# The u and gate projections of a two-block model by one level of Strassen's scheme on one NeuronCore

## What is computed

```python
h = rms_norm(x, norm_gain[l])
proj = jnp.einsum('bsd,de->bse', h, w_in[l])          # 1024 -> 4352
q, k, v, z_attn, u_ssm, z_ssm, g = jnp.split(proj, SPLITS, axis=-1)
g_attn, g_ssm = jnp.split(g + b_gate[l], N_BRANCHES, axis=-1)
attn = windowed_gqa(q, k, v, ...) * jax.nn.silu(z_attn)
y = s5_bidirectional(u_ssm, ...)                       # 32 groups of 16 channels, state 64
y = gelu(y); y = y * sigmoid(y @ w_glu + b_glu); ssm = y * silu(z_ssm)
merged = sigmoid(g_attn) * (attn @ w_branch_attn) + sigmoid(g_ssm) * (ssm @ w_branch_ssm)
```

## Time and profile before

| | us |
|---|---|
| time, median of 3 runs (lowest to highest) | 3565.43 (3548.24 to 3568.06) |
| span of the profiled execution | 3566.1 |
| PE busy | 3443.9 (97%) |
| DVE busy | 1675.5 (47%) |
| ACT busy | 1038.4 (29%) |
| POOL busy | 1101.7 (31%) |
| mean granted clock of PE | 0.988 |

### The profile page before, as it was taken

The page is one execution under the profiler, slowest core; times in us unless marked ns, Lnnn a source line. Parts: engine busy times, 40 slices in busy tenths (PEclk is TensorE's granted clock), DMA queues, the critical chain, the costliest instruction groups (busy, mean ns, idle before and its releaser), DMA issues.

```text
span 3566.1 us, 32570 instructions
## 1 busy us (share of the span) xinstructions
PE 3443.9 (97%) x11216; PEld 1789.2 (50%) x11216; DVE 1675.5 (47%) x3818; ACT 1038.4 (29%) x2575; POOL 1101.7 (31%) x1493
## 2 busy tenths in 40 slices
PE   6999899999999999999999999999999996999998
PEld 5744455555544644444444444555665443444443
DVE  5675633334365474325565556754454554222222
ACT  3221222211110362002234445643332222222222
POOL 1477777400000393000000001765561101443442
PEclk9999999999999999999999999999999998999999
DMA  4234445433245112222221000000102225968885
GB/s 162 78 105 160 145 156 163 141 125 109 96 176 178 52 37 83 88 106 102 71 96 36 24 12 12 1 1 1 71 24 76 98 96 201 355 195 264 256 251 137
DMA packets 122506, 404.74 MB, mean 113 GB/s; under 512 B 20246, under 2 KB 47766, under 8 KB 107967
## 3 DMA queue, kind: packets, MB, share of 16 engines
q1 hardware_dynamic: 85036, 228.52, 18.7%
q0 software_dynamic: 31392, 153.50, 13.8%
q10 hardware_dynamic: 5904, 20.56, 1.6%
HBM read 340.28 MB, written 117.42 MB: 128 GB/s over the span
## 4 chain that ended last, share of the span: by engine, by line
PE 84%; DVE 9%; DMA 3%; ACT 3%; issue 1%; POOL 0%; SPq 0%; DVEq 0%; POOLq 0%; ACTq 0%
PE pst L142 65%; PE pst L147 6%; DVE arena L164 5%; PE pst L2294 3%; PE pst L2389 3%; PE pst L2297 2%; DMA pwd<-arena 2%; PE pst L1354 1%; PE pst L1269 1%; PE pst L828 1%; DVE arena L167 1%; DVE arena L170 1%; ACT arena L153 1%; ACT arena L1295 0%; PE pst L2536 0%
## 5 line engine op out<-in xcount | busy, mean ns | idle before, releaser
L142 PE MATMUL pst<-arena 128*128 128x512 f32 (+4 forms) x6570 | 2688.4, 566 | 11.0 <-ACT arena L153 3.8
L142 PEld LDWEIGHTS pst<-arena 128*128 128x128 f32 x6570 | 1242.5, 195 | 1285.8 <-issue 1217.4
L164 POOL TENSOR_TENSOR arena<-arena 128x4 f32<-128x4 f32 (+7 forms) x784 | 401.8, 512 | 81.4 <-DVE arena L2098 20.9
L164 DVE TENSOR_TENSOR arena<-arena 128x512 f32<-128x512 f32 (+9 forms) x791 | 377.9, 478 | 84.2 <-ACT arena L2335 20.4
L147 PE MATMUL pst<-arena 128*128 128x128 f32 x2144 | 321.7, 284 | 56.6 <-DVE arena L256 15.3
L147 PEld LDWEIGHTS pst<-arena 128*128 128x128 f32 x2144 | 255.6, 145 | 232.5 <-issue 151.7
L1322 POOL TENSOR_SCALAR arena<-arena 128x384 f32<-128x384 f32 (+1 forms) x128 | 151.4, 1200 | 543.1 <-DVE arena L1314 541.7
L2278 POOL TENSOR_SCALAR arena<-arena 128x512 f32<-128x512 f32 (+3 forms) x160 | 218.7, 1386 | 147.5 <-DVE arena L164 137.1
L153 ACT ACTIVATE arena<-pst,arena 128x128 f32<-128x128 f32 (+1 forms) x630 | 232.0, 465 | 95.7 <-PE pst L147 93.2
L167 DVE TENSOR_SCALAR arena<-arena 128x1 f32<-128x1 f32 (+9 forms) x605 | 164.0, 271 | 178.3 <-DMA arena<-in_bc 79.5
L152 ACT ACTIVATE arena<-pst 128x512 f32<-128x512 f32 (+4 forms) x250 | 124.6, 518 | 323.9 <-PE pst L142 197.5
(11 more groups left out here) (214 smaller groups left out, 2245.3 us busy)
## 6 DMA issues: line engine op xcount, KB each, us to landing
arena<-in_w_ada SPq DMA_DIRECT2D x48, 512.0 KB, 4.8
rotd<-arena POOLq DMA_DIRECT2D x32, 512.0 KB, 4.0
arena<-rotd SPq DMA_DIRECT2D x32, 512.0 KB, 4.6
arena<-sgd SPq DMA_DIRECT2D x16, 1024.0 KB, 6.9
arena<-pwd SPq DMA_DIRECT2D x32, 416.0 KB, 5.8
arena<-in_x SPq DMA_DIRECT2D x18, 512.0 KB, 4.4
pwd<-arena SPq DMA_DIRECT2D x16, 576.0 KB, 6.1
h2d<-arena SPq DMA_DIRECT2D x17, 512.0 KB, 2.9
```

Of the source, the lines that this page charges most:

```text
L142: x = t.do.matmul(o, l, r, start=(i == 0), stop=(i == len(pairs) - 1))
L164: own(v, s).tensor_tensor(o, a, b, op).then_inc(*inc(s, *event))
```

## The change

Weights of u and gates are laid out together (2560 columns, `w_ug`, ten pieces of 256 columns x 1024 rows). A round q of the new loop takes one such piece and a pair of token tiles (512 tokens of either half of the sequence): its 2 x 2 blocks of halves are multiplied with seven products of 4 matmuls (`te_st_product`) in place of eight. There are SQ = 20 rounds: ten for the first pair of token tiles and ten for the second. DVE makes four sums of weights in a round (S1 to S4), once for each pair of token tiles 16 sums of tokens (T1 to T3, N4, in TS), and the five additions that join the products (u2, u3, c22, c12, c21). ACT copies P1 (p1), evicts the first output block and does what was done for the gates. The first two pieces of each ten are u: it is stored to `ud` in memory, ordered by token place, and loaded into Ug by 32 DMAs of SP (`sp_ug`), which replaces the 64 transposes. The blocks of the norm are now done in the order 0, 2, 1, 3, the last three between the products of rounds 0 and 1. The parameters, the eight passes of `ve_mat` (each cut in three steps) and the lag steps stand as side steps 2q and 2q + 1 in DVE's round (`ve_side`). MAT_AT gives the first side step of each pass; the lag of a pass follows one round after its end. Banks 0 to 5 hold products, 6 and 7 the side work. In S5 only the 32 z tiles are left as filler: one at its start, 29 over its 128 places, two at its end.

```diff
-PRE, PRE2 = 64, 32
-LAG_AT = [0, 4, 9, 14, 18, 22, 27]
+SP_, UT = 10, 4
+SQ = 2 * SP_
+MAT_AT = [8, 11, 15, 18, 22, 25, 29, 32]
...
+        def te_st_product(t, q, name):
...
+            if name in FIRST:
+                t.wait_ge(*st_bank_free(q, i))
+            if name == "P2":
+                t.wait_ge(*at("st_ac", "p1", q))
+            if name == "P3":
+                t.wait_ge(*at("st_ve", "S4", q))
+                t.wait_ge(*at("st_ve", "c22", q))
+            if name == "P4":
+                t.wait_ge(*at("st_ve", "u3", q))
+                t.wait_ge(*at("st_ve", "N4", c, 3))
...
+        def te_st(t):
+            te_norm_first(t)
+            for q in range(SQ):
+                te_st_product(t, q, "P1")
+                if q == 0:
+                    te_st_product(t, q, "P2")
+                    te_norm(t, 2, 0, 8)
+                if q == 1:
+                    te_norm(t, 3, 0, 2)
+                te_st_product(t, q, "P5")
+                if q == 1:
+                    te_norm(t, 3, 2, 4)
+                te_st_product(t, q, "P6")
+                if q < 2:
+                    te_norm(t, (1, 3)[q], (0, 4)[q], (2, 6)[q])
+                te_st_product(t, q, "P7")
+                if q < 2:
+                    te_norm(t, (1, 3)[q], (2, 6)[q], (4, 8)[q])
+                if q:
+                    te_st_product(t, q, "P2")
+                te_st_product(t, q, "P3")
...
+                te_st_product(t, q, "P4")
...
+                if q == 1:
+                    te_bias_row(t)
+                if q in (2, 3):
+                    te_bias(t, q - 2)
+                if q in LAG_AT:
+                    te_lag(t, LAG_AT.index(q))
...
+            for q in range(SQ):
...
+                ve_st_u2(v, q)
...
+                ve_st_c22(v, q)
...
+                if q == SP_ - 1:
+                    ve_st_T1(v, 1, 0, 4)
+                    ve_st_T2(v, 1, 0, 4)
+                    ve_st_T3(v, 1)
+                if q + 1 < SQ:
+                    ve_st_sums(v, q + 1)
+                ve_side(v, 2 * q)
+                ve_st_c12(v, q)
...
+                ve_st_c21(v, q)
...
+                if q == SP_ - 1:
+                    ve_st_T4(v, 1)
+                ve_side(v, 2 * q + 1)
...
+        def ve_side(v, s):
+
+            if s == 1:
+                ve_bias(v)
+            if s == 2:
+                ve_prm_angle(v)
+            if s == 4:
+                ve_prm_coef(v)
+            if s == 5:
+                ve_prm_powers(v)
+            if s == 6:
+                ve_prm_turns(v, 0, 6)
+            if s == 7:
+                ve_prm_turns(v, 6, 11)
+            for q4 in range(8):
+                if s == 2 * LAG_AT[q4] + 2:
+                    ve_lag(v, q4)
+            for q4 in range(8):
+                if 0 <= s - MAT_AT[q4] < 3:
+                    ve_mat(v, q4, s - MAT_AT[q4])
...
+        def sp_ug(s):
+
+            for m in range(4):
+                for c in range(2):
+                    for j in ((1, 2), (3, 0))[m % 2]:
+                        s.wait_ge(*at(f"st_pg{j}", "st", SP_ * c + m // 2))
+                s.wait_ge(*at("st_pe", ("P5", "P6", "P7", "P4")[m], SQ - 1))
                 for k in range(8):
...
+        LAG_AT = [(m + 2) // 2 + 1 for m in MAT_AT]
...
+            for i in range(4 * G + 1):
+                acc += 1 if i == 0 else 29 / (4 * G)
```

More of the change, by code:

```diff
@@ L292, in build @@
-        Ug = reg(64, G, 256)
[L293 to L319, removed]
@@ new lines, in tok, with st_bank, st_released, st_bank_free @@
+        def tok(c, half):
+            return slice(1024 * half + 512 * c, 1024 * half + 512 * c + 512)
+        def st_bank(q, i):
+            return bank((4 * q + i) % 6)
+        def st_released(q, i):
+            return at("st_ac", "C11", q) if i == 0 else at("st_ve", ("c12", "u2", "c21")[i - 1], q)
+        def st_bank_free(q, i):
+            n = 4 * q + i - 6
+            if n >= 0:
+                return st_released(n // 4, n % 4)
+            return hT_evac(2, 6) if n == -4 else hT_evac(2, 7) if n == -3 else hT_evac(2, n + 4) if n > -3 else hT_evac(0, n + 6)
@@ new lines, in ac_st_out @@
+        def ac_st_out(a, q, j):
+            c, i = q // SP_, 2 * (q % SP_) + (1, 0, 0, 1)[j]
+            u = c + 2 * (1, 0, 1, 0)[j]
+            o = OUTS[j]
+            if j == 1:
+                a.wait_ge(*at("st_pe", "P2", q))
+                a.wait_ge(*at("st_pg1", "st", q - 1))
+            else:
+                a.wait_ge(*at("st_ve", ("c22", "", "c12", "c21")[j], q))
+            if i < UT:
+                if j == 1:
+                    acopy(a, st_out(q, j), st_in(q, st_bank(q, 0))).then_inc(*inc("st_ac", "C11", q))
+                    a.wait_ge(*at("st_ac", "C11", q))
+                a.do.dma_start(ud[i * 128:i * 128 + 128, :, u * 64:u * 64 + 64],
+                               o.rearrange("p (t n) -> p t n", t=8)).then_inc(*dma(f"st_pg{j}", "st", q))
+                return
+            gi = i - UT
+            a.wait_ge(*at("prm_ve", "bgc"))
+            a.do.activation(o, st_bank(q, 0) if j == 1 else o, ACT.Tanh, scale=0.5, bias=bgc[:, gi:gi + 1]
+                            ).then_inc(*(inc("st_ac", "C11", q) if j == 1 else inc("st_ac")))
+            own(a, "st_ac").activation(o, o, ACT.Copy, scale=0.5, bias=0.5).then_inc(*inc("st_ac", "half", q, j))
+            a.wait_ge(*at("st_ac", "half", q, j))
+            a.do.dma_start(sgd[gi][:, u * 512:(u + 1) * 512], o).then_inc(*dma(f"st_pg{j}", "st", q))
@@ L380, in ac_bias_row @@
[L380 to L387 removed]
+            a.wait_ge(*at("side_pe", "brow"))
+            a.do.activation(brow, bank(6)[0:8, :], ACT.Copy, scale=-1.0).then_inc(*inc("side_ac", "brow"))
@@ L389, in po_bias, with ac_bias @@
+        def ac_bias(a, half):
+            a.wait_ge(*at("st_bias", "bias", half - 1))
+            for h in range(4 * half, 4 * half + 4):
+                a.wait_ge(*at("side_pe", "bias", h))
+                acopy(a, biasB[:, h % 4, :], bank(6 + h % 2)[:, 0:384]).then_inc(*inc("side_ac", "bias", h))
+            a.wait_ge(*at("side_ac", "bias", 4 * half + 3))
+            a.do.dma_start(biasd[:, 4 * half:4 * half + 4, :], biasB).then_inc(*dma("st_bias", "bias", half))
         def po_bias(p):
-            p.wait_ge(*at("norm_pe", "hT", 3, 7))
@@ L907, in late_tiles @@
                 made.append(now)
-            made[-1] += range(n, 16 * len(PARTS))
+            made[-1] += range(n, 96)
             return made
@@ L913, in te_s5 @@
         def te_s5(t):
-            te_lag(t, 7)
             te_s5_first(t, 0)
```

601 lines of the change are left out of this document (372 added, 229 removed).

## The result

The changed kernel took 3587.35 us (median of 7 runs, 3582.12 to 3599.25), the kernel before 3565.80 beside it (7 runs): ratio 1.0073, interval 1.0049 to 1.0097. It is slower, by 21.6 us at the medians and by 14.3 us between the spans of the profiled executions (3580.4 against 3566.1). The profiled execution of the changed kernel was the fastest of its seven, of which four lie at 3582 to 3587 and three at 3596 to 3599. After 1000 us the two traces do the same work in the same time; the last tile of S5, 976.53 before, stands at 990.03, so 13.5 of the 14.3 us arise before it.

A forecast was written before the change was run, and what follows sets the result against it. PE's work was taken to bound the kernel. 83.5 us saved, less 2.8 (start), 34 (holds), 7 (clock) and 19 (S5), gave 20.7 us faster, 3544.7 us; range 3508 to 3590.

The forecast's parts named there:

- Start: Norm blocks between products of rounds 0 and 1: PE idles 7 and 4 us; 2.8 us lost, rounds end at 98.5.
- Products: u and gates: 560 matmuls in place of 640, 68.7 us off PE; a product takes 3.44 us.
- rival (d): A product is dearer than 4 x 0.859 us; 3575 or so, chance 0.03.
- Holds in rounds 2 to 19: Late DVE holds PE in rounds 3, 5, 9 and 12: 6.3, 7.5, 9.5, 10.7; sum 34 us, bounds 10 and 60.
- 6.6 + 27.1 - 26.7 - 0.7 = 6.3 held: Round 3: DVE's adds and the parameter chain do not fit in the round, so PE is held 6.3 us.
- Clock: Four PE holds of 6 to 11 us lower its clock afterwards: 7 us lost, bounds 0 and 12.
- Start of S5: PE idle 8.5 us, 7.1 before: SP's last 8 Ug loads wait for the last product, then pwd is loaded.
- The Ug loads of the first three quarters lie beside the products P6, P7, P2, P3 and P4 of the last round: Last round: 17 us of products cover these loads; without cover each quarter costs 1.4 us, together 4.2.
- S5 loop: Half the filler: group pitch near 10 us; uncovered turns over ACT's copy cost 14 us, the first group 5.6.
- rival (c): S5 is bound by its own chain: pitch 10.6 ends the gain (3566), 11 gives 3580; chance 0.15.
- (b): DVE becomes the bound through ld_bc waits in side steps: 3596; gain gone from 49 us of holds; chance 0.15.
- rival (a): The cover holds: holds 10 us, clock 2, S5 12, start 2; 57.5 us faster, 3508; chance 0.25.

The follow-up runs named there:

- experiment 3: Changed kernel with the second half of the bias matmuls behind round 4 in place of round 3: 3582.14 us, ratio 1.0046.
- experiment 1: Changed kernel with eight Ug loads ahead of the last lag store, the other 24 spread four to a group over S5: 3557.33 us, ratio 0.9973.
- experiment 2: Changed kernel with only the last lag store moved behind the Ug loads, which stay in one piece: 3578.53 us, ratio 1.0035.
- experiment 4: Changed kernel with ACT's copies of the bias banks ahead of outputs c12 and c21 of the same round: 3572.04 us, ratio 1.0021.
- experiment 5: Changed kernel with SP issuing the in_bc load right after QA, ahead of the three stores of the pass: 3567.73 us, ratio 1.0009.

## Why the prediction was wrong

The forecast was 20.7 us faster; the spans say 14.3 slower, 35.0 apart. I line its terms up at two points of PE's timeline. They put the end of the last product at 98.5 + 432.9 (18 rounds of 24.05) + 5.2 (bias) + 16.3 (lags) + 34 + 7 = 593.9, and the last tile at 976.5 - 20.7 = 955.8. Measured: 608.5 and 990.0. The text said near 597, which is what its terms give counted from the earlier trace rows (417.3 + 32 tiles of 6.87 - 83.5 + 2.8 + 34 + 7 = 597.4); 2 of the 2.8 are clock that the 98.5 leaves out. By that count 3.5 us fewer arise before the last product and 3.5 more in the S5 loop. The whole and the idle at the start of S5 are the same in both.

- **Start**: rounds 0 and 1 end at 101.5, not 98.5: 3.0. The waits for the norm's rows were 8.14 (POOL's row, until 50.13) and 4.06 (until 75.62) against 7 and 4, so the mechanism was right; the experiments, with the same code there, pass that second point up to 3.0 us earlier, so most of this term is the spread of executions.
- **Products**: right, 3.45 us each against 3.44. 68.7 us did leave PE's work; rival (d) fell.
- **Holds in rounds 2 to 19**: 38.3 us against 34, but for other reasons. The step that failed is "6.6 + 27.1 - 26.7 - 0.7 = 6.3 held" for round 3. DVE's lateness was right (experiment 3 shows 6.05). What I had costed was only PE's wait for c22, and never who else waits for c12 and c21: ACT, with the bias copies behind them. That cost 4.20 and 13.54, where 6.3 were foreseen. The three other holds came at P3 of the rounds named, at 7.41, 6.54 and 6.38 against 7.5, 9.5 and 10.7; 10.51 us of waiting for in_bc stood before the first of them and 12.02 before the last. Why the last two came smaller I did not test.
- **Clock**: what 507 us hold beyond 432.9 + 5.2 + 16.3 + 38.3 is 14.3, against 7. Most of it is the clock, mean 0.95 there: what follows each hold, against 3.45 us a product and 1.4 for half of the bias matmuls, took 2.4 and 1.4 us longer behind the two at the bias and 3.1, 1.5 and 3.2 behind the three at P3, 11.6 together. The matmuls of the bias row, 1.0 us in no term, and small ends are the rest. The term was mis-sized: it took some 1.7 us for a hold from the earlier trace rows, and counted four holds for five. Behind the hold at 250.99 the clock was 0.50 or 0.68 for 7 us of full work.
- **Start of S5**: 29.4 us idle against 8.5, 20.9 of the 34.2. The failed step is "The Ug loads of the first three quarters lie beside the products P6, P7, P2, P3 and P4 of the last round". SP reached sp_ug only at 601.5, since sp_lag(7) before it waits for a step of DVE that stands in the last round; I had named that SP "stands in sp_ug" and not asked what it passes on its way there. And the price of 1.4 us for a quarter of loads was too low: eight took 5.88 in experiment 1 and 3.7 in experiment 2, 32 in a row 26.06, and pwd behind them landed 10.2 to 16.2 us after its issue. Experiment 2 had the order that the prediction had in mind, and the idle was still 20.64: so order and price both failed.
- **S5 loop**: 1.3 better than forecast (2.2 worse by the other count). The turns over ACT cost 11.3 in 17 groups against 14 in 16.5, the y matmuls waited 6.2 against 5.6 for the first group, and the pitch of 10.1 against 10 left rival (c) no room.

3.0 + 4.3 + 7.3 + 20.9 - 1.3 = 34.2 us; 0.8 of the 35.0 lie behind the last tile.

Of the rivals, (b) came nearest with its time (3596; the span was 3580.4) with the right kind of place, DVE's lateness and SP's late loads, but not the size: the holds were 38 us and not the 75 of its sum. Its own condition, that the gain is gone from 49 us of holds, was not met in the rounds (38.3); it was with the idle at the start of S5, which no rival held. The range ended at 3590, 2.7 above the median. With three queue orders and the place of 29 tiles changed, the same scheme gives 3511.4, close to rival (a): the count of the arithmetic was sound, and the queues spent it.

## What to carry to other kernels

When work is taken off the bound engine, walk each in-order queue (here SP and ACT) from the last place at which it surely runs to the instruction that the bound engine needs, and list every wait in between: a late producer costs by all that is queued behind whoever waits for it, not only by its own consumer. Price a block of small loads by its issue and by the landing of the load behind it; take the price of a DVE step from a row in which POOL does what it will do beside it; and put the loads that the next stage opens with ahead of those that it needs later. Through the clock, the holds on TensorE cost here a quarter to six tenths more than their idle time (2.1 us on 8.3 in experiment 4, 5.8 on 9.9 in experiment 5, 11.6 on 38.3 in the changed kernel).

## What the runs showed of the hardware that I had not expected

- 32 loads of 128 KB each to 16 partitions (1 KB runs) took 26.06 us to issue, 0.81 each, though their median issue was 0.454: one took 5.07. The first 16 took 8.90. SP's issue itself is held once enough is in flight. That is my reading; the runs show the durations.
- A load of 416 KB landed 5.8 us after its issue (median) before the change, 11.7 behind the block of 32 in the changed kernel, with the DMA engines at a full share (1.09) in that stretch, and 16.9 in experiment 2, with a weight load of 2048 KB beside it.
- The nine operations of the second pass's first step took DVE 5.21 us with POOL busy half of the time and 10.05 with POOL busy throughout: the same step at twice the price.
- The Trainium skill (TensorE: Matmul & The Clock Gate, the section on the clock gate) has idleness throttle and activity release. The changed kernel agrees. Behind the hold of 13.54 us the clock stayed at 0.50 for 3.2 us and was 0.96 in the next 2.8 (below); behind that of 7.41 us it was 0.50 for 4 us and 0.68 for 3 more. The longer hold did not cost more than the shorter one: 1.4 against 3.1 us.

```profile
175.00:178.20 3.20, 2.96 (x5) 1.75 (x6) 2.75 (x14) 1.06 (x3) 0.00 (x0) 0.50 1.02 300
178.20:181.00 2.80, 2.80 (x7) 1.25 (x7) 2.42 (x12) 0.49 (x1) 0.00 (x0) 0.96 0.72 298
```
